# The even mixer as one stage of fourteen weight units, with compression in 32 products

## What is computed

```python
def even_mixer(h, w_in, w_out, gm_w_s, gm_b, cmp_pe, cmp_w1, cmp_w2):
    z = h @ w_in
    u, v, q, kc, vc, ks, vs, kw, vw, gl = jnp.split(z, cuts, axis=-1)
    out_a = gmlp_spatial_gate(heads(u, 8), heads(v, 8), gm_w_s, gm_b)
    out_b = nsa_attention(rope(heads(q, 8)), heads(kc, 2), heads(vc, 2), rope(heads(ks, 2)),
                          heads(vs, 2), rope(heads(kw, 2)), heads(vw, 2), gl, cmp_pe, cmp_w1, cmp_w2)
    return jnp.concatenate([out_a, out_b], axis=-1) @ w_out

def gmlp_spatial_gate(u, v, w_s, b):      # v normalised over the 64 of a head
    s = einsum('hts,bcshd->bcthd', w_s * causal, normed(gelu(v))) + b
    return gelu(u) * s

def nsa_compress(t, pe, w1, w2, idx):     # 15 blocks of 32 tokens, stride 16
    blocks = t[:, idx] + pe[:, None, :]
    return gelu(blocks.reshape(..., 32 * 64) @ w1) @ w2
```

## Time and profile before

| | us |
|---|---|
| runs, median of 3 | 3627.48 |
| lowest, highest | 3625.56, 3632.71 |
| profiled execution | 3624.22 |
| its span | 3622.4 |
| even mixer within the span, 225.7 to 499.6 | 273.9 |

### The profile page before, as it was taken

The page is one execution under the profiler, slowest core; times in us unless marked ns, Lnnn a source line. Parts: engine busy times, 40 slices in busy tenths (PEclk is TensorE's granted clock), DMA queues, the critical chain, the costliest instruction groups (busy, mean ns, idle before and its releaser), DMA issues. The chain is left out here.

```text
span 3622.4 us, 59069 instructions
## 1 busy us (share of the span) xinstructions
PE 3291.9 (91%) x23248; PEld 3021.1 (83%) x23248; DVE 2260.4 (62%) x2575; ACT 1809.1 (50%) x2251; POOL 204.0 (6%) x112
## 2 busy tenths in 40 slices
PE   6997689999989799889898998897899999999997
PEld 6997479898679798889797988894899988999995
DVE  3451344577854646664546556653788888888885
ACT  3441334433234345555343454642777777777773
POOL 0000100000410101010101010100000000000000
PEclk9996689999999899999899999997999999999999
DMA  4541045544235443333454433342799999999993
GB/s 162 184 175 47 1 151 186 185 178 162 82 122 184 165 152 128 128 129 140 151 185 141 150 129 128 117 152 82 292 343 346 342 342 342 347 346 345 344 344 126
DMA packets 97046, 702.37 MB, mean 194 GB/s; under 512 B 10880, under 2 KB 11008, under 8 KB 12928
## 3 DMA queue, kind: packets, MB, share of 16 engines
q1 hardware_dynamic: 96896, 700.26, 52.7%
HBM read 699.16 MB, written 1.05 MB: 193 GB/s over the span
## 5 line engine op out<-in xcount | busy, mean ns | idle before, releaser
L819 PE MATMUL ps<-act_high,weight_low 128*128 128x256 f32 x3120 | 893.0, 286 | 0.0
L819 PE MATMUL ps<-act_high,weight_high 128*128 128x256 f32 x2736 | 792.5, 290 | 43.5 <-DVE act_low L424 22.5
L819 PE MATMUL ps<-act_low,weight_high 128*128 128x256 f32 x2736 | 784.3, 287 | 0.0
L819 PE MATMUL ps<-weight_low,act_high 128*128 128x256 f32 (+1 forms) x2400 | 685.5, 286 | 0.0
L819 PE MATMUL ps<-weight_high,act_high 128*128 128x256 f32 (+1 forms) x2240 | 652.4, 291 | 21.4 <-DVE weight_low L895 10.5
L819 PE MATMUL ps<-weight_high,act_low 128*128 128x256 f32 (+1 forms) x2240 | 639.7, 286 | 0.0
L819 PEld LDWEIGHTS ps<-act_high,weight_low 128*128 128x128 f32 x3120 | 609.6, 195 | 0.0
L819 PEld LDWEIGHTS ps<-act_high,weight_high 128*128 128x128 f32 x2736 | 535.8, 196 | 55.0 <-DVE act_low L424 20.2
L819 PEld LDWEIGHTS ps<-act_low,weight_high 128*128 128x128 f32 x2736 | 535.9, 196 | 2.1
L819 PEld LDWEIGHTS ps<-weight_low,act_high 128*128 128x128 f32 x2400 | 463.9, 193 | 5.8 <-issue 1.0
L819 PEld LDWEIGHTS ps<-weight_high,act_high 128*128 128x128 f32 x2240 | 432.6, 193 | 35.0 <-issue 21.6
(11 more groups left out here) (439 smaller groups left out, 5275.5 us busy)
## 6 DMA issues: line engine op xcount, KB each, us to landing
ring<-in_l_w_in SPq DMA_DIRECT2D x90, 1024.0 KB, 4.8
ring<-in_l_moe_up SPq DMA_DIRECT2D x56, 1024.0 KB, 6.0
ring_more<-in_l_moe_gate SPq DMA_DIRECT2D x56, 1024.0 KB, 4.9
ring_more<-in_l_moe_up SPq DMA_DIRECT2D x56, 1024.0 KB, 6.0
vtm<-in_l_moe_down SPq DMA_DIRECT2D x56, 1024.0 KB, 4.8
merged<-in_l_moe_gate SPq DMA_DIRECT2D x55, 1024.0 KB, 4.9
ring<-in_l_moe_down SPq DMA_DIRECT2D x55, 1024.0 KB, 4.8
ring<-in_l_ffn_down SPq DMA_DIRECT2D x43, 1024.0 KB, 4.8
```

The costliest lines, as they stand in the source:

```text
L819: ins = nc.tensor.matmul(out, still[a], moving[b], start=first and n == 0, stop=last and n == 2, skip_group_check=True)
```

## The change

The six stage functions go, and `even_stage` does all of the mixer in one block, with fourteen weight units through three raw buffers: 0 kc and vc, 1 and 2 q, 3 ks and kw, 4 vs and vw, 5 gl (192 columns wide in all, not 2048), 6 and 7 v, 8 and 9 u, 10 and 11 the output weights of the gate's half, 12 and 13 those of attention's half. An output unit multiplies four chunks of input with 512 columns, in matmuls of 512 columns; its input is split in pairs of chunks.

- Keys are stored once; two DMAs within SBUF copy them to the other half of the partitions (`swapped`).
- Compression: k and v of both groups and the 16 positions pe stand in one buffer `kv`, the odd tokens shifted to the other 64 partitions by two DMAs (`shifted`). One product then takes two positions, both groups and pe, 34 columns from 128 rows; 32 products in all. The compressed keys are rotated with the rotation matrix, and are made on both halves at once. `w1` is 1 MB, and is loaded into `merged` with the tables, in the stage before.
- Rotation takes three pairs of chunks, each behind the product that makes it.
- Attention's twelve branches are slots: in slot s TensorE makes score s, transposes branch s - 2 and attends branch s - 3, which adds up in one bank for each group. Scores have one pair of banks, probabilities three buffers. The branches come as in `BRANCHES`: of group 0 two with 128 keys, two with 256, two with 15, and then of group 1.
- Between the slots lie the gate's products (`mix`, behind slot 3) and output unit 10 (behind slot 5); units 11 to 13 follow the last slot.

The new functions, cut; VectorE's and ScalarE's steps have the same arithmetic as those of before (line lengths are indented less than in the file):

```diff
@@ split_ffn_stage, SP @@
-                sp.dma_start(tables[0], tables[1]).then_inc(tables_loaded.sem, 16)
+        for dst, src in tables:
+            sp.dma_start(dst, src).then_inc(tables_loaded.sem, 16)
@@ project_stage, rope_stage, attention_stage, load_stage, gmlp_stage, compress_stage go; in their place: @@
+KV, QN, KN, VSN, GLN, VN, UN_, EA, EB, EVEN_UNITS = 0, 1, 3, 4, 5, 6, 8, 10, 12, 14
+GATES = 24
+BRANCHES = [(g, qt, b) for g in range(2) for qt, b in ((0, 1), (0, 2), (1, 1), (1, 2), (0, 0), (1, 0))]
+PASSED = len(BRANCHES)
...
+def even_stage(c, norm, units, e, then):
...
+    def load(n):
+        if n >= 3:
+            sp.wait_ge(low.sem, low.base + n - 2)
+        sp.dma_start(raws[n % 3][:, 0:width(n)], units[n]).then_inc(loaded[n % 3].sem, 16)
+    for n in range(2, 5):
+        load(n)
+    sp.wait_ge(taken.sem, taken.base + KV + 1)
+    sp.dma_start(kv[HD:P, :, 0, 0:T], kv[0:HD, :, 0, 1:T + 1]).then_inc(shifted.sem, 16)
+    sp.dma_start(kv[0:HD, :, 1, 1:T + 1], kv[HD:P, :, 1, 0:T]).then_inc(shifted.sem, 16)
+    for n in range(5, 8):
+        load(n)
+    sp.wait_ge(roped.sem, roped.base + 3)
+    sp.dma_start(k[HD:P, 2:4, :], k[0:HD, 0:2, :]).then_inc(swapped.sem, 16)
+    sp.dma_start(k[0:HD, 2:4, :], k[HD:P, 0:2, :]).then_inc(swapped.sem, 16)
+    for n in range(8, EVEN_UNITS):
+        load(n)
+    ahead.sync(sp, [low.base + EVEN_UNITS - 2, low.base + EVEN_UNITS - 1])
...
+    def cmp_hidden():
+        pe.wait_ge(filled.sem, filled.base + 1)
+        pe.wait_ge(shifted.sem, shifted.base + 32)
+        pe.wait_ge(taken.sem, taken.base + KV + 1)
+        for m in range(2):
+            dst = ps[0:HD, 6, 34 * m:34 * m + 34].rearrange("p (g n) -> p g n", g=2)
+            for l in range(16):
+                last = nc.tensor.matmul(dst, e.w1[:, m, l, :], kv[:, m, :, 2 * l + 1:2 * l + 258:CMP_STRIDE],
+                                        start=(m == 0 and l == 0), stop=(l == 15), skip_group_check=True)
+        last.then_inc(hidden.sem, 1)
...
+    def score(n):
+        g, qt, b = BRANCHES[n]
+        nk = keys(n)
+        if n == 0:
+            pe.wait_ge(roped.sem, roped.base + 3)
+            pe.wait_ge(swapped.sem, swapped.base + 32)
+        else:
+            pe.wait_ge(biased.sem, biased.base + n)
+        if b == 0:
+            pe.wait_ge(ready.sem, ready.base + 1)
+        for p in range(2):
+            half = slice(HD * p, HD * p + HD)
+            right = e.kT[half, g, 0:NCMP] if b == 0 else k[half, b - 1 if p == g else b + 1, 0:nk]
+            for j in range(2):
+                last = nc.tensor.matmul(ps[:, 2 + p, T * j:T * j + nk], q[half, 2 * g + j, P * qt:P * qt + P],
+                                        right, start=True, stop=True)
+        last.then_inc(scored.sem, 1)
+    def turn(n):
+        pe.wait_ge(weighted.sem, weighted.base + n + 1)
+        if n:
+            pe.wait_ge(probs_taken.sem, probs_taken.base + n)
+        for l in range(slabs(n)):
+            for a in range(4):
+                last = nc.tensor.transpose(ps[0:rows(n), 4 + l, P * a:P * a + P],
+                                           S[n % 3][:, a, P * l:P * l + rows(n)], c.ident)
+        last.then_inc(probs.sem, 1)
+    def attend(n):
+        g, qt, b = BRANCHES[n]
+        pe.wait_ge(probs_taken.sem, probs_taken.base + n + 1)
+        if n == 0:
+            pe.wait_ge(ready.sem, ready.base + 1)
+        for p in range(2):
+            for j in range(2):
+                for l in range(slabs(n)):
+                    at = 512 + P * (b - 1) + HD * g
+                    still = e.vT[:, g, :] if b == 0 else c.vtm[:, l, at:at + HD]
+                    last = nc.tensor.matmul(
+                        ps[HD * p:HD * p + HD, 6 + g, T * j + P * qt:T * j + P * qt + P], still,
+                        probs_sb[n % 2][0:rows(n), l, 2 * p + j, :],
+                        start=(n % 6 == 0 and j == 0 and l == 0), stop=(n % 6 >= 4 and l == slabs(n) - 1),
+                        skip_group_check=True)
+        last.then_inc(attended.sem, 1)
+    def slot(s):
+        if s < PASSED:
+            score(s)
+        if 0 <= s - 2 < PASSED:
+            turn(s - 2)
+        if 0 <= s - 3 < PASSED:
+            attend(s - 3)
+    norm.tensor(pe)
+    project(KV)
+    project(QN)
+    project(QN + 1)
+    cmp_hidden()
+    rope_turn(0)
+    project(KN)
+    rope_turn(1)
+    cmp_second()
+    project(VSN)
+    rope_turn(2)
+    cmp_rotate()
+    project(GLN)
+    project(VN)
+    project(VN + 1)
+    project(UN_)
+    slot(0)
+    project(UN_ + 1)
+    for s in range(1, PASSED + 3):
+        slot(s)
+        if s == MIX:
+            mix()
+        if s == OUT:
+            out(EA, 0)
+    out(EA + 1, 0)
+    out(EB, 2)
+    out(EB + 1, 4)
...
+    norm.scalar_start(act)
+    make_high(1)
+    norm.scalar(act)
+    for n in range(EA):
+        unload(n)
+        make_high(n + 2)
+        if n == QN + 1:
+            cmp_gelu()
+    act.wait_ge(var_made.sem, var_made.base + 1)
+    nc.scalar.activation(mean(2), mean(1), ACT.Sqrt).then_inc(root_made.sem, 1)
+    for s in range(PASSED + 2):
+        if s < PASSED:
+            exps(s)
+        if s >= 2:
+            take_probs(s - 2)
+        if s == MIX + 2:
+            for i in range(2):
+                gm_split(i)
+        if s == OUT + 2:
+            make_high(EB)
+        if s == 9:
+            att_split(0)
+    att_split(1)
+    make_high(EB + 1)
+    act.wait_ge(made.sem, made.base + EB + 1)
+    ahead.scalar(act)
+    first_root(c)
...
+    norm.vector(dve)
+    for n in range(1, 5):
+        make_low(n)
+    cmp_take_pe()
+    rope_add(0)
+    make_low(5)
+    rope_add(1)
+    cmp_keep()
+    make_low(6)
+    rope_add(2)
+    cmp_rope()
+    for n in range(7, 10):
+        make_low(n)
+    gm_stats()
+    make_low(10)
+    bias(0)
+    gm_norm()
+    make_low(11)
+    for s in range(1, PASSED + 1):
+        factor(s - 1)
+        if s < PASSED:
+            bias(s)
+        if s == MIX + 1:
+            for b in range(2):
+                gm_gate(b)
+        if s == MIX + 2:
+            for i in range(2):
+                gm_split(i)
+        if s == OUT + 2:
+            add_x(EA, 0)
+            make_low(EB)
+        if s == 9:
+            att_split(0)
+    att_split(1)
+    make_low(EB + 1)
+    add_x(EA + 1, 0)
+    add_x(EB, 2)
+    ahead.vector(dve, high.base + EVEN_UNITS + 1)
+    add_x(EB + 1, 4)
...
+MIX, OUT = 3, 5
...
@@ even_mixer @@
-    project_stage(c, [
...
-    load_stage(c, [(c.ring[:, 0:2, :].rearrange("p m n -> p (m n)"), d["l_cmp_w1"])])
-    gmlp_stage(c, seg[:, 0:4], vtm[:, :, 0:512], c.cat[:, 0:4], wT, bias, causal)
-    compress_stage(c, seg[:, 12:14], w1, w2, pe_cols, ccos, csin, kT, vT)
-    rope_stage(c, seg[:, 4:12], rot64, cos, sin)
...
-    attention_stage(c, groups, HD ** -0.5)
+    wide = [d["l_even_units"][n] for n in range(EVEN_UNITS - 1)]
+    even_stage(c, Rms(c, c.gains[:, KD:2 * KD]), wide[:GLN] + [d["l_even_gates"]] + wide[GLN:], EvenTables(c),
+       then=[d[n][d[n].shape[0] // 4] for n in ("l_ffn_gate", "l_ffn_up")])
```

848 lines of the change are left out of this document (333 added, 515 removed).

## The result

The changed kernel takes 3519.91 us (median of 4 runs, 3519.21 to 3524.51), the kernel before took 3628.82 beside it: a ratio of 0.9706, with a 95% interval of 0.9694 to 0.9718. The forecast was 3533.4, the range 3519 to 3551. So the sign and the size are as forecast, with 13.5 us more gained than the sum gave. It is a narrow hit: the time lies 0.9 us above the lower end of the range, and nearer to the full-clock rival's 3522.3 than to the forecast. The profiled execution took 3519.46 us, its span 3517.7.

A forecast was written before the change was run, and what follows sets the result against it. Behind TensorE-bound input products, chains between engines and the long compression were taken to bound the mixer. Stretches ending at 405.5 gave 179.8 us for 273.9, so 3627.5 - 94.1 = 3533.4 us, range 3519 to 3551.

The forecast's parts named there:

- full-clock rival: The fourteen attention slots run at TensorE's full clock: 64.9 us, 11.1 less, for 3522.3 us in all; chance 0.18.
- Norm to first product: Stage start, from the norm to the first input unload: same instructions as before, first product covered better by chunks; 12.2 us.
- Input products: First to last input unload, ten products with compression, rotations and half-clock stretches between them: 64.1 us, ending at 302.0.
- Loads and copies: Table and w1 loads, key and value copies, queued weight loads: all covered by other work, costing nothing.
- Into the slots: From last input unload to second branch's mask and maximum: an uncovered ScalarE and VectorE chain, TensorE almost idle, 9.9 us.
- Slots: Fourteen attention slots, walked at 79.2 us at half clock and 64.9 at full; 76 taken, nearest to half clock.
- Handovers: Rival: one more engine handover on the chain per slot, 9 us, plus 14 elsewhere: 3547.5 us; chance 0.16.
- dear compression: Rival: compression records cost by columns and rows, so the 64 take 29 us, not 3.9: 3559 us; chance 0.02.
- unhidden weights: Rival: every wide unit waits for its own load in SP's queue, 9.0 us more each: 3651 us; chance 0.02.
- The rest of the span: Everything outside the mixer stage must stay as it was, to within 1 us, or the sum rests on a wrong picture.
- Output: Stage end: three remaining output units at 5.5 us each, 16.5, plus last add and next norm's start 1.0; to 405.5.
- Rules weighed: Trace preferred over two skill rules: no 1.38 us drain per table load, and the clock falls though TensorE is never idle.

The follow-up runs named there:

- late mask: Against the changed kernel, GpSimd's multiplication of the causal mask into the gate's weights moved from the stage's start to just ahead of the third rotation product; 3519.53 us, stage 167.9.

## Why the prediction was right, and where it was off

- **Norm to first product, 12.2, measured 14.7.** Wrong by 2.5: the step "the same instructions" did not look at GpSimd, where the change had put a multiplication. The late mask gave these 2.5 back: 1.4 in the scalings, the rest by the earlier clock.
- **Input products, 64.1, measured 61.6.** The wide ones, the gates and compression (3.9 for 4.07) hold. The half clock that I put behind compression (0.8) was not there, the one behind the gates was partly. That this error of 2.5 the other way cancels the norm's is luck: in the kernel with the late mask the same stretch took 63.2, with the half clock around the gates' product longer. The slip of 0.3 did not come: ScalarE waited for TensorE before every unload.
- **Loads and copies at nothing.** Held: no high part waited for a load in this stage.
- **Into the slots, 9.9, measured 9.6.** Held, with TensorE idle for 7 us in it.
- **Slots, 76, measured 67.2.** This is the step that made the sum 9 us too long. The term that was mis-sized is TensorE's: "attend 4 × 0.95" for 256 keys at half clock and "4 × 0.61" for 15 keys. I took the price of products that write one half in a row, but the new order writes both, and they overlap. 2.88 for 3.8 and, at half clock in the kernel with the late mask, 1.12 for 2.44. The tail holds two of each: 12.5 us in the sum, 8.0 by the measured half-clock prices, 6.0 with the clock rising at its end. Slots 4, 5 and 7 gave 4.8 more, where the clock was rising or at 1.00 and I had gone through at half. The steps of ScalarE and VectorE (4.8, 5.2, 13.9, 9.6, each within 0.7) held; slot 10 took 6.1 for 5.2, for the negation behind GpSimd. The walk had given 79.2, of which I had taken off 3.2 for a clock in between.
- **The full-clock rival.** Its 64.9 us lie nearer to 67.2 than my 76, but the clock was 0.70 in the slots, which between the levels 0.50 and 1.00 is 0.50 for three fifths of the time. It would have been right by its number and not by its reason: a slot of 256 keys takes 5.12 us at either level, and in the tail the higher clock gave 2 us.
- **Handovers, dear compression, unhidden weights.** The last two did not come. Of the first, one came that I had not seen, slot 10's negation, at 0.9 us of the rival's 9; another was found where I put one in (unit 11 behind its add).
- **The rest of the span.** I had written that it must stay to within 1 us. It did not: 2.5 us shorter behind the stage, 2.4 of them in a stage that has both lengths, 198 and 200.5, in kernels that do not edit it. By my own sign the sum was in doubt. The clock of that stage was 0.97 before and 0.99 after, over the same 1340 records of TensorE. The rest of the span makes 1.6 us of the 13.5.
- **Output, 17.5, measured 17.7.** Held: 5.4 to 5.7 a unit.
- **Rules weighed.** The root's load again starts as the split ends and its activation follows at once, with exp's load behind it; ScalarE, kernel after:

```profile
303.42 1.90 ACT L1085 ACTIVATE weight_high<-ring_more 128x2048 fp32r<-128x2048 f32 x1
305.33 1.28 ACT L1146 ACT_TABLE_LOAD   x1
306.63 0.22 ACT L1146 ACTIVATE small<-small 128x16 f32<-128x16 f32 x1
306.86 1.28 ACT L1122 ACT_TABLE_LOAD   x1
308.16 0.40 ACT L1122 ACTIVATE work<-work,stats 128x128 f32<-128x128 f32 x1
```

  No drain of the 1.38 us that the Trainium skill ("ScalarE: Activation LUTs", What ACT_TABLE_LOAD costs) adds. The clock's fall in the fully busy gates' product came again, too.

## What to carry to other kernels

Where many stages become one, read each engine's list against each other's, GpSimd's also: an instruction that moves beside another engine's work can change both. Order products with 64 columns of weights so that the two halves of the output take turns; four and four in a row cost half as much again as in turn. Put a wide unit into a chain of slots in pieces of a pause's length, with whatever each piece waits for a full slot ahead; whole, it costs on the chain what it saves behind.
